# Hybrid encoder trunk on one core: w_out in half tiles inside the attention blocks, top-k rounds in pairs, an earlier S5 and GLU, and no unread matmuls in the last block

## What is computed

```
proj = h @ w_in                               # q, k, v, index q/k/w, u
# attention, 4 query blocks of 128 rows, 8 heads of 64, one shared k/v
score = sum_h w_h * relu(qi_h . ki) ; masked to keys of admissible chunks
idx   = top_k(score, 128)
p     = softmax(q_h . k[idx] / 8) ; attn = p @ v[idx]
# S5 state-space model on u, 32 groups of 16 channels, 64 complex states
y = gelu(s5(u)) ; y = y * sigmoid(y @ glu_w + glu_b)
mixed = concat(rms_norm(attn), rms_norm(y))   # 512 + 512 columns
x = x + gate2 * (mixed @ w_out)
```

## Time and profile before

| what | value |
|---|---|
| median of 3 runs | 2172.32 us (2168.12 to 2175.24) |
| the profiled execution's own time | 2174.77 us |
| its span, first to last instruction | 2172.8 us |
| TensorE busy | 2066.5 us, 95% |
| VectorE busy | 1347.1 us, 62% |
| ScalarE busy | 706.7 us, 33% |
| mean granted TensorE clock | 0.951 |

### The profile page before, as it was taken

The page is one execution under the profiler, slowest core; times in us unless marked ns, Lnnn a source line. Parts: engine busy times, 40 slices in busy tenths (PEclk is TensorE's granted clock), DMA queues, the critical chain, the costliest instruction groups (busy, mean ns, idle before and its releaser), DMA issues.

```text
span 2172.8 us, 25378 instructions
## 1 busy us (share of the span) xinstructions
PE 2066.5 (95%) x9564; PEld 1666.1 (77%) x9564; DVE 1347.1 (62%) x2099; ACT 706.7 (33%) x1066; POOL 243.1 (11%) x219
## 2 busy tenths in 40 slices
PE   6999899999689999999999999999978999999998
PEld 5788778877467788888888877888755678888887
DVE  5768846567884664543467787466688646555334
ACT  3332222342434432222342322234234433222123
POOL 0006900300000000000000294040000000000000
PEclk8999999999669999999999999999986799999999
DMA  7475556342110263533347364553330024454332
GB/s 261 126 214 179 161 147 179 97 113 69 49 39 11 87 202 118 187 97 104 88 125 223 119 196 131 156 146 101 88 88 20 20 59 158 143 165 128 114 90 75
DMA packets 395985, 264.77 MB, mean 122 GB/s; under 512 B 56560, under 2 KB 371672, under 8 KB 395864
## 3 DMA queue, kind: packets, MB, share of 16 engines
q1 hardware_dynamic: 386784, 259.89, 40.1%
q10 hardware_dynamic: 9080, 3.26, 0.7%
HBM read 254.98 MB, written 6.29 MB: 120 GB/s over the span
## 4 chain that ended last, share of the span: by engine, by line
PE 76%; DVE 14%; issue 5%; ACT 3%; DMA 1%; ACTq 0%; SPq 0%; DVEq 0%; POOL 0%; POOLq 0%
PE ps L1650 22%; PE ps L1651 22%; PE ps L1652 22%; DVE w_lo L990 3%; DVE mod_acc L1011 2%; DVE score L1367 2%; DVE small L1365 2%; PE ps L1910 1%; PE ps L1929 1%; ACT w_hi L684 1%; PE ps L1937 1%; PE ps L1920 1%; DVE x L1096 1%; DMA stage<-in_ffn_w 1%; PE ps L1858 1%
## 5 line engine op out<-in xcount | busy, mean ns | idle before, releaser
L1650 PE MATMUL ps<-h_hi,w_hi 128*128 128x512 f32 x1728 | 687.4, 398 | 17.7 <-DVE w_lo L990 13.8
L1651 PE MATMUL ps<-h_lo,w_hi 128*128 128x512 f32 x1728 | 679.4, 393 | 0.0
L1652 PE MATMUL ps<-h_hi,w_lo 128*128 128x512 f32 x1728 | 679.1, 393 | 0.0
L990 DVE TENSOR_TENSOR w_lo<-stage,w_hi 128x1024 fp32r<-128x1024 f32 (+2 forms) x322 | 394.4, 1248 | 103.2 <-ACT w_hi L684 99.3
L1650 PEld LDWEIGHTS ps<-h_hi,w_hi 128*128 128x128 f32 x1728 | 327.5, 190 | 99.0 <-issue 16.4
L1652 PEld LDWEIGHTS ps<-h_hi,w_lo 128*128 128x128 f32 x1728 | 328.1, 190 | 70.0
L1651 PEld LDWEIGHTS ps<-h_lo,w_hi 128*128 128x128 f32 x1728 | 328.0, 190 | 65.7 <-issue 0.5
L684 ACT ACTIVATE w_hi<-stage 128x1024 fp32r<-128x1024 f32 (+2 forms) x322 | 318.7, 1016 | 173.1 <-PE ps L1652 164.9
L1650 PE MATMUL ps<-g_hi,w_hi 128*128 128x512 f32 x704 | 276.4, 393 | 2.4 <-DVE g_lo L1303 2.4
L1651 PE MATMUL ps<-g_lo,w_hi 128*128 128x512 f32 x704 | 274.2, 389 | 0.0
L1652 PE MATMUL ps<-g_hi,w_lo 128*128 128x512 f32 x704 | 274.1, 389 | 0.0
(11 more groups left out here) (300 smaller groups left out, 1859.1 us busy)
## 6 DMA issues: line engine op xcount, KB each, us to landing
stage<-in_ffn_w SPq DMA_DIRECT2D x210, 512.0 KB, 4.6
mod_stage<-in_mod_w SPq DMA_DIRECT2D x144, 512.0 KB, 5.5
stage<-in_ffn_w SPq DMA_DIRECT2D x64, 448.0 KB, 4.0
stage<-in_w_in SPq DMA_DIRECT2D x20, 512.0 KB, 4.0
mod_first<-in_mod_w SPq DMA_DIRECT2D x16, 512.0 KB, 9.3
stage<-in_w_out SPq DMA_DIRECT2D x16, 512.0 KB, 4.2
x_in<-in_x SPq DMA_DIRECT2D x4, 512.0 KB, 5.4
stage<-in_w_in SPq DMA_DIRECT2D x8, 256.0 KB, 4.0
```

The costliest lines, as they stand in the source:

```text
L990: V.tensor_tensor(w_lo[:, c % RING, 0:n], stage[:, c % RING, 0:n], w_hi[:, c % RING, 0:n].bitcast(F32), ALU.subtract).then_inc(w_split_lo. ...
L1650: mm(out, hi, rhs_hi, start=first, stop=False)
L1651: mm(out, hi, rhs_lo, start=False, stop=False)
L1652: return mm(out, lo, rhs_hi, start=False, stop=last)
```

## The change

w_out is loaded as half tiles: a chunk holds the y rows (m0+16 to m0+19) or the attention rows (m0+20 to m0+23) of two column tiles. The y halves of tiles 0 to 3 run in turns 19 to 22 and are added to x by an update of their own in turns 20 to 23; those of tiles 4 to 7 run after turn 31. The GLU moves from turns 8 to 15 (6 matmuls each) to turns 4 to 7 (12 each), and all that follows it moves too. Top-k rounds of two blocks alternate; eight rounds stand in t = 9 to 11, and 40 in turns 0 to 23. `keep_streaming` starts at turn 32, so it never runs. S5 states run at t = 4, 5, 6, 8 and outputs at t = 5, 6, 7, 9; `s5_scan` waits for single results. All four gelus run ahead of turn 0.

```diff
-STATES_AT = {5: 0, 6: 1, 9: 2, 10: 3}
-Y_AT = {7: 0, 8: 1, 10: 2, 11: 3}
+STATES_AT = {4: 0, 5: 1, 6: 2, 8: 3}
+Y_AT = {5: 0, 6: 1, 7: 2, 9: 3}
-GELU_AT = {2: 2, 4: 3}
-S5_LO_AT = {1: 0, 2: 1, 4: 2, 6: 3}
-GLU_AT = {8 + 2 * n + j: (n, j) for n in range(ST) for j in range(2)}
-TANH_AT = {10 + 2 * n: n for n in range(ST)}
-ROOT_AT, BCAST_AT = 20, 21
-SSM_AT = {24: (0, 1), 25: (2, 3)}
-SSM_LO_AT = {26: (0, 1), 27: (2, 3)}
+GELU_AT = {10: (0, 1), 11: (2,)}
+S5_LO_AT = {0: 0, 1: 1, 2: 2, 3: 3}
+GLU_AT = {4 + n: n for n in range(ST)}
+TANH_AT = {5 + n: n for n in range(ST)}
+ROOT_AT, BCAST_AT = 12, 13
+SSM_AT = {15: (0, 1), 16: (2, 3)}
+SSM_LO_AT = {17: (0, 1), 18: (2, 3)}
+HALF_AT = {19 + n: n for n in range(EARLY_OUT)}
+HALF_X_AT = {20 + n: n for n in range(EARLY_OUT)}
-KEEP_FROM = 22
-TOPK_EARLY = {11: 5}
-TOPK_AT = {e: 2 if e < 19 else 1 for e in range(3 * HEADS)}
-OUT_SPLIT_AT = {10: 16, 12: 17, 15: 18, 17: 19}
+KEEP_FROM = NA_STEPS
+TOPK_WITH = [(1, 2)] * HEADS + [(2, 3)] * HEADS + [(3,)] * HEADS + [()] * HEADS
+OUT_SPLIT_AT = {6: 16, 8: 17, 10: 18, 12: 19, 21: 20, 23: 21}
...
@@ weights
-                return tiles(a["w_out"], layer, 0, KT, (m - 16) * P)
+                if m < 20:
+                    return tiles(a["w_out"], layer, AT, ST, (m - 16) * 2 * P, 2 * P)
+                return tiles(a["w_out"], layer, 0, AT, (m - 20) * 2 * P, 2 * P)
@@ SyncE: u8 has three buffers
+                            if 8 <= m < 12:
+                                u_store(l, m - 8)
+                            if 9 <= m < 12:
+                                u_fetch(l, m - 9)
+                            if m in (12, 13, 14, 16):
+                                y = min(m - 12, ST - 1)
+                                y_store(l, y)
+                                if y == 0:
+                                    u_fetch(l, 3)
+                                y_fetch(l, y)
@@ ScalarE
                 act.wait_ge(*h_done.at(l, 2 * KT - 1))
-                for m in range(2):
-                    act.wait_ge(*y_in[m].at(l, 16 * 2 * GI - 1))
-                    gelu(m)
+                gelu(3)
+                for m in range(ST):
+                    gelu_high(m)
...
                 att_square(QB - 1)
+                split_hi(l, m0 + 22)
                 att_high(QB - 1)
+                split_hi(l, m0 + 23)
                 for n in range(KT):
-                    if n < KT - 2:
-                        split_hi(l, m0 + 20 + n)
+                    if n in (2, 4):
+                        split_hi(l, m0 + 23 + n // 2)
@@ VectorE, t = 2 to 11
                     split_lo(l, m0 + t + AHEAD)
+                    if t in (10, 11):
+                        for _ in range(2):
+                            topk_max(1)
+                            topk_take(1)
@@ VectorE, turn e
+                    blocks = TOPK_WITH[e]
+                    if blocks:
+                        topk_max(blocks[0])
                     mask_head(e)
+                    if len(blocks) > 1:
+                        topk_max(blocks[1])
+                    if blocks:
+                        topk_take(blocks[0])
                     if b:
                         att_step(b - 1, h)
...
-                    for _ in range(TOPK_AT.get(e, 0)):
-                        topk_round(TOPK_BLOCK[rounds])
-                        rounds += 1
...
+                    if len(blocks) > 1:
+                        topk_take(blocks[1])
...
+                    if e in HALF_X_AT:
+                        n = HALF_X_AT[e]
+                        mix_update(n, 4 + n % 2, half_even, m0 + 16 + n // 2)
@@ VectorE, after turn 31
+                split_lo(l, m0 + 22)
                 att_step(QB - 1, 6)
                 att_step(QB - 1, 8)
+                split_lo(l, m0 + 23)
                 for n in range(KT):
-                    if n < KT - 2:
-                        split_lo(l, m0 + 20 + n)
+                    if n in (2, 4):
+                        split_lo(l, m0 + 23 + n // 2)
@@ TensorE, turn e
                     if e in GLU_AT:
-                        glu(*GLU_AT[e])
+                        glu(GLU_AT[e])
+                    if e in HALF_AT:
+                        y_half(HALF_AT[e])
                     if e >= KEEP_FROM:
-                        keep_streaming(3, m0 + 16)
+                        keep_streaming(3, m0 + 19)
@@ TensorE, after turn 31
                 values(NA - 1)
-                for n in range(3):
-                    out_half(n, AT, KT)
+                for n in range(EARLY_OUT, KT - 1):
+                    y_half(n)
                 att_turn(QB - 1)
                 pe.wait_ge(*att_n.at(l, QB - 1))
-                out_half(3, AT, KT)
+                y_half(KT - 1)
                 pe.wait_ge(*att_done.at(l, QB - 1))
                 for n in range(KT):
-                    if n >= 4:
-                        out_half(n, AT, KT)
-                    out_half(n, 0, AT)
+                    att_half(n)
```

More of the change, by code:

```diff
@@ L179, in __call__, with mark, need @@
         self.eng.wait_ge(self.sem, self.base + self.n)
+    def mark(self, i):
+        i.then_inc(self.sem, 1)
+        self.n += 1
+        return self.base + self.n
+    def need(self, value):
+        self.eng.wait_ge(self.sem, value)
 def trunk(nc, a):
@@ L1439, in s5_scan @@
                     half = (slice(0, NS), slice(NS, P))
-                    step(*(V.tensor_tensor(hs[half[g], 0, :, g, 1:J + 1], X[0][half[g]], M[0][half[g]], ALU.subtract) for g in range(2)),
-                         V.tensor_tensor(hs[half[0], 1, :, 0, 1:J + 1], X[1][half[0]], M[1][half[0]], ALU.add))
+                    step.need(re)
+                    step.mark(V.tensor_tensor(hs[half[0], 0, :, 0, 1:J + 1], X[0][half[0]], M[0][half[0]], ALU.subtract))
+                    step.mark(V.tensor_tensor(hs[half[1], 0, :, 1, 1:J + 1], X[0][half[1]], M[0][half[1]], ALU.subtract))
+                    step.need(im)
+                    step(V.tensor_tensor(hs[half[0], 1, :, 0, 1:J + 1], X[1][half[0]], M[1][half[0]], ALU.add))
                     V.tensor_tensor(hs[half[1], 1, :, 1, 1:J + 1], X[1][half[1]], M[1][half[1]], ALU.add).then_inc(hs_done.sem, 1)
@@ L1632, in _ @@
                 power(l, 1)
-                for b in range(2):
+                att_power(0)
+                power(l, 2)
+                for b in range(1, QB):
                     att_power(b)
-                power(l, 2)
-                att_power(2)
-                att_power(3)
                 power(l, 3)
@@ L1949, in glu @@
                         i = split3(ps[:, 4 + n % 2, :], w_tile(c, k), h_hi[:, AT + k, :], h_lo[:, AT + k, :], k == 0, k == ST - 1)
[L1950 to L1965 removed]
+                    i.then_inc(w_used.sem, 1)
@@ new lines, in half_tile, with y_half @@
+                def half_tile(c, k, z):
+                    s = slice((2 * k + z) * P, (2 * k + z + 1) * P)
+                    return w_hi[:, c % RING, s], w_lo[:, c % RING, s]
+                def y_half(n):
+                    c = m0 + 16 + n // 2
+                    if n % 2 == 0:
+                        chunk_ready(l, c)
+                    if 2 <= n < 6:
+                        pe.wait_ge(*x_new.at(l, NP * KT + n - 2))
+                    bank = 4 + n % 2 if n < EARLY_OUT else OUT_BANK[n - EARLY_OUT]
+                    for k in range(ST):
+                        if n == 0:
+                            pe.wait_ge(*mix_done.at(l, k))
+                        i = split3(ps[:, bank, :], half_tile(c, k, n % 2), h_hi[:, AT + k, :], h_lo[:, AT + k, :],
+                                   k == 0, n < EARLY_OUT and k == ST - 1)
+                    if n % 2:
+                        i.then_inc(w_used.sem, 1)
+                    elif n < EARLY_OUT:
+                        i.then_inc(half_even.sem, 1)
@@ new lines, in att_half @@
+                def att_half(n):
+                    c = m0 + 20 + n // 2
+                    if n % 2 == 0:
+                        chunk_ready(l, c)
+                    if n in (2, 3):
+                        pe.wait_ge(*x_new.at(l, NP * KT + EARLY_OUT + n - 2))
+                    bank = n % 2 if n < EARLY_OUT else OUT_BANK[n - EARLY_OUT]
+                    for k in range(AT):
+                        i = split3(ps[:, bank, :], half_tile(c, k, n % 2), h_hi[:, k, :], h_lo[:, k, :],
+                                   n < EARLY_OUT and k == 0, k == AT - 1)
+                    i.then_inc((out_even, w_used)[n % 2].sem, 1)
```

179 lines of the change are left out of this document (93 added, 86 removed).

## The result

The changed kernel takes 2155.99 us (median of four runs, 2153.65 to 2157.19), the kernel before 2171.28 us in the same session (2168.12 to 2175.24). The ratio is 0.9927, with a 95% interval of 0.9908 to 0.9947: faster by 0.7%. Forecast were 2179 us and no change to speak of. The time lies in the range and 4 us from rival B's, and it is B that happened: the clock fell in one layer and held in the other.

What follows compares the result with a forecast made beforehand. TensorE, busy 95% of the span, was taken as the bound, with VectorE setting the pace in places. Per layer 0.5 - 4.0 + 10.9 + 2.5 - 6.5 = +3.4 us, giving 2179 us; range 2138 to 2189.

Steps and rivals of the forecast that it cites:

- rival B: Block 3: the clock falls in one layer only, -12 us in all, 2160 us; chance 0.19.
- Does the clock hold in block 3?: Block 3: light matmuls don't count fully towards the clock; with a 1.4 us gap at turn 24 it falls to 1.2 GHz.
- Rival C: Block 3: the clock holds in both layers, -31 us in two layers, 2141 us; chance 0.25.
- Rival A: Block 3: the clock falls at turn 24 in both layers, +3.4 us a layer, 2179 us; chance 0.50.
- Step 1: Projections ahead of turn 0: shorter top-k tail used up by S5 waits and a later split, +0.5 us a layer.
- Step 2: Blocks 0 to 2: paired top-k rounds save VectorE time, y halves cost TensorE time, -4.0 us a layer.
- Step 3: Block 3 at the full clock: turns without unread matmuls take 2.43 us, plus gaps, -5.6 us a layer.
- Step 3': Block 3 at the low clock: turns take 4.7 us, +10.9 us a layer; y halves behind it add +2.5.
- Step 4: w_out: VectorE's loop sets the stage, 40.2 us instead of 46.7, -6.5 us a layer.
- Rival D: w_out: its gain isn't there, through delayed norm steps or TensorE stalls in turns 20 to 23; 2192 us, chance 0.06.

Runs made afterwards that it cites:

- split21_late: The changed kernel with the high part of w_out chunk 21 made in turn 27 instead of 23, no unread matmuls: 2136.8 us, ratio 0.9840.
- gap_more: The changed kernel with one more ScalarE pass over weight chunk 21 in turn 23, doubling TensorE's gap at turn 24: 2173.8 us, ratio 0.9999.
- before_no_unread: The kernel before the change with its unread matmuls taken out and nothing else changed: 2181.1 us, ratio 1.0035.
- serial_rounds: split21_late with the two top-k rounds of a turn in blocks 0 and 1 one after the other instead of interleaved: 2145.8 us, ratio 0.9877.
- fill_tail: split21_late with 28 unread matmuls in the wait behind w_out in each layer: 2131.4 us, ratio 0.9804.
- shift kernels: The changed kernel with 4, 8 or 12 unread matmuls ahead of turn 22 in each layer: 2170.2, 2174.3 and 2176.4 us.
- shift_12: The changed kernel with 12 unread matmuls ahead of turn 22 in each layer: 2176.4 us, ratio 1.0026.
- halves_in_block3: split21_late with the four early y halves in turns 24 to 27 instead of 19 to 22, chunks 20 and 21 split in turns 26 and 28: 2154.4 us, ratio 0.9920.

## Why the prediction was wrong, point by point

**The step that failed is "Does the clock hold in block 3?"**, and the chances put on it. It took two things together, that the light stream doesn't count towards the clock and that there is a gap at turn 24, and concluded that the clock would fall in both layers. The experiments part them. The stream holds 2.4 GHz by itself (split21_late); the gap makes the clock fall, mostly but not always (seven of eight at 1.07 to 1.08 us). The stretch from 626 to 650, from which the light stream was judged, was read for more than it shows: it shows turns that didn't bring the clock back, which is so again in gap_more (28.10 us busy at 0.50), and says nothing on whether they keep it. Even on the first point there is an exception close by. The kernel before regains 2.4 GHz 1.1 us ahead of its first unread matmul, behind a broadcast of eight matmuls of 128 columns:

```profile
651.33 1.91 PE L1735 MATMUL ps<-ident,small 128*128 128x128 f32 x8
...
654.19 0.91 PE L1910 MATMUL ps<-k_t,q_t 64*128 64x384 f32 x2
655.03 0.96 PE L1937 MATMUL ps<-w_hi 128*128 128x512 f32 x3
```

The logits at 654.19 take 0.91 us for the 1.65 of the turns before. Layer 2 and both layers of before_no_unread rise at the same point, so the unread matmuls didn't raise the clock. Rival C's own condition ("if the stream of block 3 at 2.4 GHz is enough by itself") was met, and a gap that ScalarE's order of work makes took half of its gain away again.

**Rival A's sum was too high as well.** The four kernels in which the clock falls in both layers come to 2168 to 2172 us when what was added to them is taken off (2170.2 - 1.7, 2174.3 - 3.4, 2176.4 - 5.1, 2173.8 - 1.9), not 2179. Had A come true, the change would have made no difference. Several steps make the difference. For a layer with a fall A summed +3.4 us. Layer 2 shows +1.7. Layer 1 would have shown -17.1 + 14.8 (block 3 low instead of high, 10.5 and 4.3) + 1.5 (w_out behind it) = -0.8. That is 1.7 (layer 2) and 4.2 us (layer 1) less than the sum. In the same order: turn 0 earlier by 0.3 and 0.9 us instead of later by 0.5, block 0 at 25.7 and 24.8 us for 25.9, block 2 at 35.3 and 34.5 for 35.4, block 3 longer by 10.5 for 10.9, and 1.5 us for the low start of the y halves instead of 2.5; against them block 1 gained 1.2 and 0.6 us less than the 5.9 forecast. The last 2.0 us lie behind the last mixer, where the change does nothing; they were in no step. 2179 - 1.7 - 4.2 - 2.0 = 2171. (A's own span, given as 2168 to 2188, adds up to 2166 at its lower end: 2179 - 9 - 4.)

**Step 1**, +0.5: -0.9 and -0.3, within the scatter of turn 0 from profile to profile (4.3 us), so neither the gain nor the waits are shown. Turn 0 waits 3.45 us for the last rotary product, not 5.87; how much of that is the shorter tail of top-k rounds wasn't tried.

**Step 2**, -4.0: -5.4 in layer 1, -3.5 in layer 2. The mechanism was right: VectorE's rounds closed up (2.6 us for a pair and a mask, as summed), the gain is in block 1, and the y halves are paid for in block 2. serial_rounds gives pairing 5.1 and 5.8 us of it in blocks 0 and 1 of the two layers (9.0 us in all between the medians).

**Step 3**, -5.6 with the clock held: -4.3. The gap was put at 1.4 us and measures 1.08, but there are two more (0.30 and 0.55 us), and turns without a gap are 2.5 to 2.6 us apart, not 2.43. **Step 3'**, +10.9: +10.5, with turns 4.65 us apart (1696.85 to 1701.50) for 4.7.

**Step 4**, -6.5: -6.6, 40.1 us for 40.2. VectorE's loop sets the stage as it was read from the earlier trace rows, and TensorE's saving turned into the wait of 6.7 us. The prediction dismissed that wait: the feed-forward "starts at 1.2 GHz already, so nothing more is lost there". fill_tail shows that the wait costs about 4 us a layer through the clock, in the kernel before most likely too, where 2.37 us stood in that place and the clock was 0.53 behind it; there it wasn't tried.

**Rival B** gave 2160 us; 2156.0 came, for B's own reason: a short gap, seen in one layer and missed in the other. That it hits so closely is partly luck. Its sums for the two layers were 1.5 and 1.7 us too high, and 2.0 us were in no step. **Rival D** didn't occur.

The Trainium skill's page "TensorE: Matmul & The Clock Gate", section Why this matters for your kernels, would have had the clock hold through gaps as short as this one, and block 3 of both layers at the full clock. The trace disagrees: a gap of 1.08 us was enough in layer 2. The same page, Part 1: The HAM clock gate, says that the chip looks at TensorE's activity on a time of its own that no kernel starts, so that one program meets it at different phases. The shift kernels fit that, since moving the gap by 0.5 to 2.3 us against the rise changed the outcome in layer 1.

## What to carry to other kernels

Ask of a light stretch of TensorE two separate questions: whether it keeps the high clock, which a stretch that runs at the low one can't tell you, and where its gaps are, since one microsecond of waiting for another engine can cost fifteen behind it. Look at what that engine does ahead of the result that TensorE waits for, and move it: a high part made four turns later was worth 19 us here, more than the whole change had brought. Matmuls that nobody reads are worth their time only where they stand in such a wait, and heavy work that could go elsewhere may be worth more where it raises the clock.

## What the runs showed of the hardware that was not expected

- The granted clock of a stretch depends on the clock with which it starts. The logits, transposes and values of block 3 kept 2.4 GHz with TensorE busy 19.15 of 20.37 us (split21_late) and stayed at 1.2 GHz with it busy 28.10 of 28.10 us (gap_more).
- The low clock of such a stream can end by itself. In the profile of shift_12 the same stream came back to 2.4 GHz after 30.6 us at 1.2 GHz with TensorE busy throughout, 1.6 us ahead of the first full matmul, in both layers; in the kernel before it came back behind eight matmuls of 128 columns (651.33), 1.1 us ahead of the first unread one.
- A gap of 1.07 to 1.08 us in that stream was followed by a fall seven times of eight, ones of 1.21 and 1.23 us in before_no_unread by one in each layer, and the gaps of 0.44 and 0.55 us in split21_late by none. Whether the eighth escaped by its moment alone stays open; the difference seen between it and the seven others is where it lay behind the last rise of the clock. A gap of 2.02 us that began at nearly the same place, 20.0 us (layer 1 of gap_more), was caught.
- In halves_in_block3 the clock stayed at 1.2 GHz over 28.75 us of light turns with TensorE busy for 27.04 us, and rose in the stretch of full matmuls that followed them.
